# Reordering one store, one router step and the final gated sums of a mixture-of-experts tail

## The chip, the cores and the metric

The kernel runs on one core of a Trainium2 chip. The metric is the device time of one execution in microseconds (us), as the median of several runs. All times inside an execution are us from the start of its span.

## The reference

The program is one step of a diffusion trunk: one layer for 640 tokens (128 context tokens and 512 latent tokens) of width 1024, in fp32. Cut to what the change touches, the last part of the layer is:

```
h = modulate(x, norm_g[1], sh2, sc2)
scores = sigmoid(h @ w_router)                  # 16 experts, in 4 groups
idx, w = top 2 experts of the best group, weights normalised
for e in range(16):
    a = silu(h @ w_exp_gate[e]) * (h @ w_exp_up[e])
    y = y + combine[:, e] * (a @ w_exp_down[e])
x = x + g2 * y
return rms_norm(x, final_norm_g)
```

Ahead of it stand the input projection, the recurrent mixer, the neighbourhood attention, the merge of the two branches and the output projection.

## The kernel before

Every product is made in three passes: each operand is split into a high part (ScalarE, a rounding copy) and a low part (VectorE or GpSimd, the value less its high part), and TensorE multiplies high by high, high by low and low by high.

**The expert stage.** The 1280 (token, expert) pairs are sorted into tiles of 128 slots, one expert for each tile: 16 tiles for the 16 experts, and as many spill tiles as the routing asks for (`more` counts them in pairs). For each tile `t` three weight blocks of 2 MB are loaded: gate (`Wg`, index 0), up (`Wu`, index 1) and down (`Wd`, index 2). There is one raw buffer of each. SyncE issues the load of a block as soon as VectorE has made the low part of the block before it in that buffer (semaphore `W_lo_ok[x]`). GpSimd gathers the 128 token rows `hS` of a tile from DRAM. TensorE transposes them (`h_cols`), ScalarE makes the high part `hSH`, VectorE the low part `hSL` (`h_low`). TensorE then runs `up(t, 0)`, the transposes of the tile before it, `up(t, 1)` and `down(t-1)`. The result of a tile is weighted on ScalarE into `Ys` (with `wslot`, the weight of each slot), and SyncE stores it to the DRAM tensor `slot_rows` (`rows_out`, semaphore `ys_out`).

**Entry of the stage.** VectorE's queue, written out by hand, makes the low part of the first up block (`weights_low(1, 0)`), then `h_low(0, 0)`, then `slot_weights` (nine small operations: the slot weights, the slot of each token's two experts, the group of each slot), then the low part of the first down block.

**End of the stage.** The last two tiles are not stored. Their weighted rows `yg` are spread to the tokens by products on TensorE with one-hot matrices `mark`. All other tiles come back by gathers on GpSimd from `slot_rows`: for each of the five token tiles `G[t]` one gather of the row of the first expert (L680), and one that adds the row of the second expert (L685). GpSimd starts them when the low parts of the last up and down blocks are made (the `G` tiles lie in that memory) and when every `Ys` has been stored:

```
        pool.wait_ge(W_lo_ok[1], 2 * more + E)
        pool.wait_ge(W_lo_ok[2], 2 * more + (E - 1))
        for b in range(2):
            pool.wait_ge(ys_out[b], 16 * more + 8 * (E - 2))
```

SyncE's own queue at the end is: the last up block's load, the store of the last-but-one `Ys`, the store of the last `Ys` (`rows_out(2 * more + (E - 3), 1)`, which waits for ScalarE), the load of the last down block into the gate's buffer (L588, so it has the name `Wg` in the profile), the two broadcasts `g2b` of the gate rows, and then `fgb`, the broadcast of the final norm's weights, which waits for `gg_ok >= 1`, the first `G` tile multiplied by its gate. The five output stores follow.

**VectorE's last queue.** `out_low` and `out_half` make the weighted rows of the last tile and their low parts in two halves of the columns, with ScalarE's `ygH` between. TensorE's `spread(t, h)` adds the residual and the last two tiles' rows in PSUM. Then, for each token tile: `gated(t)` multiplies `G[t]` by the gate (it waits for both gathers of tile `t`), `summed(t)` adds PSUM, ScalarE squares and sums the row and takes the root, and `normed(t)` takes the reciprocal, scales by `fgb` and releases the store of the tile. `residual(4)` on TensorE reuses a PSUM bank and waits for `summed(0)`. SyncE and VectorE each work strictly through their queues in order: a wait holds everything behind it.

Of the kernel before, what the change touches and what calls it, by code (L numbers as in the profile page):

```python
# [32 lines left out]
TT = T // P  # L33
# [20 lines left out]
E, TOPK, SP_G = 16, 2, 4  # L54
# [53 lines left out]
def build(nc, xT, cT, w_ada, w_ada_late, b_ada, norm_g, final_g, wtiles, par_in, pack, biasd, w_router, r_bias,  # L108
# [15 lines left out]
    def sem(name):  # L124
        return ctx.enter_context(nc.semaphore(name))
# [220 lines left out]
    gg_ok, yg_ok, yh_ok, yl_ok, oc_mm = sem("gg_ok"), sem("yg_ok"), sem("yh_ok"), sem("yl_ok"), sem("oc_mm")  # L346
# [49 lines left out]
    def spill_pairs(engine):  # L396

        engine.wait_ge(idx_ok, 2)
        return engine.value_load(eI[0:1, NT:NT + 1], min_val=0, max_val=SPILL // 2)
# [32 lines left out]
    def _(sp):  # L432
# [131 lines left out]
        def rows_out(t, b):  # L564
            sp.wait_ge(ys_ev, t + 1)
            sp.dma_start(yd[bass.ds(t * P, P), :], Ys[b][:]).then_inc(ys_out[b], 16)

        def of_tile(t):
            return sp.value_load(eI[0:1, bass.ds(t, 1)], min_val=0, max_val=E - 1)

        def step(s, b, expert_of):
            load(0, s + 2, expert_of(s + 2))
            load(1, s + 2, expert_of(s + 2))
            if not (isinstance(s, int) and s == 0):
                load(2, s + 1, expert_of(s + 1))
                rows_out(s - 1, 1 - b)
# [4 lines left out]
        more = spill_pairs(sp)  # L581
        with nc.sync.Fori(0, more + (E // 2 - 2)) as j:
            for b in range(2):
                step(2 * j + 2 + b, b, of_tile)
        rows_out(2 * more + (E - 3), 1)
        sp.wait_ge(W_lo_ok[0], 2 * more + E)
        sp.sem_inc(ticks, 1)
        sp.dma_start(Wraw[0][:], experts[bass.ds(of_tile(2 * more + (E - 1)), 1), 2]  # L588
                     .rearrange("o p (k f) -> (o p) k f", k=KT)).then_inc(W_in[0], 16)

        sp.wait_ge(u_mm, 2 * more + (E - 1))
        sp.wait_ge(gb_in, 32)
# [813 lines left out]
    def _(dve):  # L1406
# [563 lines left out]
        def slot_weights():  # L1970

            dve.wait_ge(inv_mm, 2)
            w0, w1, w2 = (PS[:, 5, 160 + i * NT:160 + (i + 1) * NT] for i in range(3))
            st(v.tensor_copy(wslot[:], w2))
            st(v.tensor_tensor(slotF[:], posF.rearrange("p x t -> p (x t)"), tilF.rearrange("p x t -> p (x t)"), ALU.add))
            st(v.tensor_scalar(early_end[:], eF[:, NT:NT + 1], 2.0 * P, (E - 2.0) * P - 0.5, ALU.mult, ALU.add))
            seq.last(2)
            st(v.scalar_tensor_tensor(wslot[:], wslot[:], 1.0 / W_STEP, w1, ALU.mult, ALU.add))
            seq.last(2)
            st(v.tensor_scalar(wrest[:], slotF[:], -1.0, float(NT * P), ALU.mult, ALU.add))  # L1980
            seq.last(1)
            v.scalar_tensor_tensor(wslot[:], wslot[:], 1.0 / W_STEP, w0, ALU.mult, ALU.add).then_inc(idx_ok, 1)
            seq.last()
            st(v.scalar_tensor_tensor(wrest[:], slotF[:], early_end[:], wrest[:], ALU.is_ge, ALU.mult))
            st(v.tensor_scalar(groupI[:], idxF[:], float(NP), None, ALU.is_ge))
            seq.last()
            v.tensor_tensor(slotI[:].rearrange("p x t -> p (x t)"), slotF[:], wrest[:], ALU.add).then_inc(slot_ok, 1)

        def weights_low(x, t):

            for k in range(0, KT, 4):
                dve.wait_ge(W_hi_ok[x], 2 * t + (k // 4 + 1))
                y = v.tensor_tensor(W_lo[x][:, k:k + 4], Wraw[x][:, k:k + 4], W_hi[x][:, k:k + 4].bitcast(F32),  # L1993
                                    ALU.subtract)
            y.then_inc(W_lo_ok[x], 1)

        def h_low(t, b):
            dve.wait_ge(ht_hi, t + 1)
            v.tensor_tensor(hSL[b][:], PS[:, 0:2, :].rearrange("p h (k c) -> p (h k) c", k=4),  # L1999
                            hSH[b][:].bitcast(F32), ALU.subtract).then_inc(ht_lo, 1)  # L2000
# [48 lines left out]
                weights_low(2, t)  # L2049

        weights_low(1, 0)
        h_low(0, 0)
        slot_weights()
        weights_low(2, 0)
        expert(0, 0)
        expert(1, 1)
# [1 line left out]
        more = spill_pairs(dve)  # L2058
# [18 lines left out]
        def gated(t):  # L2077

            dve.wait_ge(gy_in[t], 32)
            v.tensor_tensor(G[t][:], G[t][:], g2b[min(t, 1)][:], ALU.mult).then_inc(gg_ok, 1)  # L2080

        def out_half(h):

            cols = slice(h * 512, (h + 1) * 512)
            dve.wait_ge(d_mm, 2 * more + (E + h))
            v.scalar_tensor_tensor(yg[1][:, cols], PS[:, 6 + h, :], ws2[:, 1:2], G2s[1][:, cols], ALU.mult, ALU.mult) \
                .then_inc(yg_ok, 1)

        def out_low(i, n, cols):

            dve.wait_ge(yh_ok, n)
            v.tensor_tensor(ygL[i][:, cols], yg[i][:, cols], ygH[i][:, cols].bitcast(F32), ALU.subtract) \
                .then_inc(yl_ok, 1)

        def summed(t):

            dve.wait_ge(oc_mm, t + 1)
            dve.wait_ge(gg_ok, t + 1)
            a = 2 * t % 8
            v.tensor_tensor(xo[t][:].rearrange("p (h c) -> p h c", h=2), PS[:, a:a + 2, :],  # L2100
                            G[t][:].rearrange("p (h c) -> p h c", h=2), ALU.add).then_inc(x2_ok, 1)

        def normed(t):

            if t == 0:
                dve.wait_ge(gb_in, 80)
            dve.wait_ge(sqo_ok, t + 1)
            st(v.reciprocal(stat[:, 10 + t:11 + t], stat[:, 5 + t:6 + t]))
            seq.last()
            v.scalar_tensor_tensor(yo[t][:], xo[t][:], stat[:, 10 + t:11 + t], fgb[:], ALU.mult, ALU.mult) \  # L2110
                .then_inc(out_ok, 1)

        out_low(0, 1, slice(0, D))
        dve.wait_ge(hs_in[1], 16 * more + 8 * E + 16)
        out_half(0)
        out_low(1, 2, slice(0, 512))
        out_half(1)
        out_low(1, 3, slice(512, D))
        for t in range(TT):
            gated(t)  # L2120
            summed(t)
            if t:
                normed(t - 1)
        normed(TT - 1)

    ctx.close()
# [89 lines left out]
```

## Time and profile before

| | |
|---|---|
| median of 3 runs | 1189.74 us (1188.63 to 1189.96) |
| time of the profiled execution | 1189.96 us |
| its span | 1188.1 us |
| TensorE matmul busy | 1128.4 us, 95% |
| VectorE busy | 914.0 us, 77% |
| ScalarE busy | 676.6 us, 57% |
| GpSimd busy | 265.2 us, 22% |
| granted TensorE clock, mean | 0.98 |
| DMA | 233.25 MB, 196 GB/s over the span |

The busy shares are means over stages that have different limits. The profiled execution's time is 1.86 us more than its span: what lies outside the span is taken as unchanged. The stages in order are the input projections and mixers, the merge and output projection, the router, the experts, and the tail of gathers and sums.

### The profile page before, as it was taken

How to read it: one execution, taken by the hardware profiler on the slowest of the kernel's cores; microseconds unless marked ns; L12 is line 12 of the kernel's file. 1: busy time of each engine (PE TensorE's matmuls, PEld its weight loads, DVE VectorE, ACT ScalarE, POOL GpSimd, SP SyncE). 2: the span in 40 equal slices, each digit the busy share in tenths (PEclk: the TensorE clock that was granted, in tenths of full speed). 3: DMA queues.
4: the chain of work that ended last, by engine and by line, in shares of the span. 5: the costliest groups of instructions: out<-in, count | busy, mean ns of one | idle time of the engine just before them, and what ended most of it. 6: DMA issues, size and time to landing. Idle time of an engine off the chain costs nothing.

```text
span 1188.1 us, 19988 instructions
## 1 busy us (share of the span) xinstructions
PE 1128.4 (95%) x7152; PEld 1029.3 (87%) x7152; DVE 914.0 (77%) x1276; ACT 676.6 (57%) x1038; POOL 265.2 (22%) x142
## 2 busy tenths in 40 slices
PE   5999999999999999999999999996899999999995
PEld 1599999999999998899999999995788888888873
DVE  5747797979788797866556655838798999999887
ACT  3646667576666757652222222436587787787753
POOL 0132122222122221133333332310111011011050
PEclk9999999999999999999999998997899999999998
DMA  9235612122121112124444435608899999999995
GB/s 367 101 98 154 197 59 81 46 77 70 66 84 58 62 57 80 41 90 142 142 142 141 141 106 213 236 18 333 300 342 403 415 424 419 424 409 411 415 318 170
DMA packets 54875, 233.25 MB, mean 196 GB/s; under 512 B 5368, under 2 KB 22048, under 8 KB 46368
## 3 DMA queue, kind: packets, MB, share of 16 engines
q1 hardware_dynamic: 50496, 216.79, 48.8%
q0 software_dynamic: 4320, 15.73, 4.0%
q8 instruction: 30, 0.49, 0.2%
q14 instruction: 29, 0.24, 0.1%
HBM read 211.50 MB, written 21.00 MB: 196 GB/s over the span
## 4 chain that ended last, share of the span: by engine, by line
PE 49%; DVE 4%; DMA 1%; issue 1%; ACT 1%; SPq 0%; DVEq 0%; ACTq 0%
PE PS L982 23%; PE PS L744 22%; PE PS L974 1%; PE PS L849 1%; PE PS L894 1%; DMA Wg<-in_experts 1%; DMA fgb<-in_final_g 1%; PE PS L995 1%; DVE hrow L1857 0%; DVE yo L2110 0%; DVE G L2080 0%; PE PS L882 0%; DVE WuLo L1993 0%; DVE WgLo L1993 0%; PE PS L900 0%
## 5 line engine op out<-in xcount | busy, mean ns | idle before, releaser
L622 POOL TENSOR_TENSOR wLo<-wRaw,wHi 128x1024 fp32r<-128x1024 f32 x80 | 202.7, 2534 | 549.5 <-ACT wHi L1095 549.5
L744 PE MATMUL PS<-hHi,wHi 128*128 128x320 f32 x896 | 285.6, 319 | 4.5 <-DVE hLo L1512 1.9
L744 PE MATMUL PS<-hLo,wHi 128*128 128x320 f32 x896 | 278.2, 310 | 0.0
L744 PE MATMUL PS<-hHi,wLo 128*128 128x320 f32 x896 | 278.1, 310 | 0.0
L744 PEld LDWEIGHTS PS<-hHi,wHi 128*128 128x128 f32 x896 | 169.9, 190 | 5.5 <-issue 5.2
L744 PEld LDWEIGHTS PS<-hLo,wHi 128*128 128x128 f32 x896 | 169.7, 189 | 0.0
L744 PEld LDWEIGHTS PS<-hHi,wLo 128*128 128x128 f32 x896 | 169.5, 189 | 0.0
L1681 DVE SCALAR_TENSOR_TENSOR acc<-adaL,csil,acc 128x512 f32<-128x512 f32 x112 | 103.9, 985 | 10.2 <-DMA adaL<-in_w_ada_late 9.7
L1095 ACT ACTIVATE wHi<-wRaw 128x1024 fp32r<-128x1024 f32 x80 | 84.1, 1051 | 45.2 <-PE PS L744 43.1
L1993 DVE TENSOR_TENSOR WgLo<-Wg,WgHi 128x2048 fp32r<-128x2048 f32 x34 | 76.3, 2287 | 15.2 <-ACT WgHi L1316 15.0
L1993 DVE TENSOR_TENSOR WdLo<-Wd,WdHi 128x2048 fp32r<-128x2048 f32 x34 | 76.3, 2287 | 8.5 <-ACT WdHi L1316 8.3
L1993 DVE TENSOR_TENSOR WuLo<-Wu,WuHi 128x2048 fp32r<-128x2048 f32 x36 | 80.8, 2285 | 1.4 <-ACT WuHi L1316 1.3
L1536 DVE TENSOR_TENSOR PtLo<-PS,PtHi 128x384 fp32r<-128x384 f32 (+1 forms) x80 | 39.6, 496 | 52.7 <-ACT PtHi L1131 52.6
L1316 ACT ACTIVATE WgHi<-Wg 128x2048 fp32r<-128x2048 f32 x34 | 63.3, 1910 | 17.4 <-DMA Wg<-in_experts 17.4
L1547 DVE TENSOR_SCALAR Sb<-Sb,prec 128x384 f32<-128x384 f32 (+1 forms) x80 | 70.6, 924 | 1.4
L1195 ACT ACTIVATE Sb<-Sb,nmax 128x384 f32<-128x384 f32 (+1 forms) x80 | 45.0, 564 | 46.5 <-DVE nmax L1559 46.4
L1316 ACT ACTIVATE WuHi<-Wu 128x2048 fp32r<-128x2048 f32 x36 | 66.9, 1909 | 3.9 <-DMA Wu<-in_experts 2.4
L1131 ACT ACTIVATE PtHi<-PS 128x384 fp32r<-128x384 f32 (+1 forms) x80 | 35.6, 445 | 57.0 <-PE PS L824 56.4
L644 POOL COPY idxc<-idxI 128x1 int32 (+1 forms) x16 | 15.1, 946 | 219.1 <-PE PS L974 219.1
L1316 ACT ACTIVATE WdHi<-Wd 128x2048 fp32r<-128x2048 f32 x34 | 63.1, 1906 | 0.3 <-DMA Wd<-in_experts 0.3
L982 PE MATMUL PS<-WgHi,hSH 128*128 128x512 f32 x144 | 57.4, 398 | 4.3 <-DVE hSL L1999 2.6
L982 PE MATMUL PS<-WuHi,hSH 128*128 128x512 f32 x144 | 57.8, 402 | 0.0
(358 smaller groups left out, 2822.6 us busy)
## 6 DMA issues: line engine op xcount, KB each, us to landing
wRaw<-in_wtiles SPq DMA_DIRECT2D x80, 512.0 KB, 3.5
Wu<-in_experts SPq DMA_DIRECT2D x18, 2048.0 KB, 9.5
Wg<-in_experts SPq DMA_DIRECT2D x18, 2048.0 KB, 10.6
Wd<-in_experts SPq DMA_DIRECT2D x17, 2048.0 KB, 10.3
adaL<-in_w_ada_late SPq DMA_DIRECT2D x32, 512.0 KB, 4.1
ada<-in_w_ada SPq DMA_DIRECT2D x8, 1024.0 KB, 17.7
slot_rows<-Ys SPq DMA_DIRECT2D x16, 512.0 KB, 11.0
slot_rows<-tab SPq DMA_DIRECT2D x12, 512.0 KB
```

What stands on the lines that cost most here:

```text
L622: nc.gpsimd.tensor_tensor(wLo[b][:], wRaw[b][:], wHi[b][:].bitcast(F32), ALU.subtract).then_inc(w_lo, 1)
L644: seq.step(nc.gpsimd.tensor_copy(idxc[b][:], idxI[:, bass.ds(t, 1)]))
L744: r = mm(PS[:, bank, 0:HALF], w[:, k, :], x[:, k, cols], start=(k == 0 and w is wHi[b] and x is xh), stop=(k == KT - 1 and w is wLo[b]))
L982: x = mm(out, lhs[l][:, k, :], rhs[r](k)[:, cols], start=(k == 0 and l == r), stop=(k == n - 1 and l == 1))
L1095: A(wHi[b][:], wRaw[b][:], ACT.Copy).then_inc(w_hi, 1)
L1131: A(PtHi[:, 0:nt, hh * P:(hh + 1) * P], PS[:, 6, 0:nt * P].rearrange("p (t q) -> p t q", q=P), ACT.Copy).then_inc(pt_hi, 1)
L1195: A(Sb[(blk + b) % 2][hh][:, 0:w], Sb[(blk + b) % 2][hh][:, 0:w], ACT.Exp, scale=-1.0, bias=nmax[hh][:], accum_out=psumr[:, hh:hh + 1]).th ...
L1316: A(W_hi[x][:, k:k + 4], Wraw[x][:, k:k + 4], ACT.Copy).then_inc(W_hi_ok[x], 1)
L1536: v.tensor_tensor(PtLo[:, 0:nt, cols], PS[:, 6, 0:nt * P].rearrange("p (t q) -> p t q", q=P), PtHi[:, 0:nt, cols].bitcast(F32), ALU.subtra ...
L1547: v.tensor_scalar(x, x, prec[:, hh:hh + 1], None, ALU.mult).then_inc(prob_ok, 1)
L1681: y = v.scalar_tensor_tensor(acc[:, g, :], w, c1, acc[:, g, :], ALU.mult, ALU.add)
L1993: y = v.tensor_tensor(W_lo[x][:, k:k + 4], Wraw[x][:, k:k + 4], W_hi[x][:, k:k + 4].bitcast(F32), ALU.subtract)
```

## The change

It moves instructions within three queues; it adds and removes no computation.

```
@@ SyncE, after the loop of the experts
-        rows_out(2 * more + (E - 3), 1)
         sp.wait_ge(W_lo_ok[0], 2 * more + E)
         sp.sem_inc(ticks, 1)
         sp.dma_start(Wraw[0][:], experts[bass.ds(of_tile(2 * more + (E - 1)), 1), 2]
                      .rearrange("o p (k f) -> (o p) k f", k=KT)).then_inc(W_in[0], 16)
+        rows_out(2 * more + (E - 3), 1)

@@ VectorE, entry of the expert stage
         weights_low(1, 0)
+        slot_weights()
         h_low(0, 0)
-        slot_weights()
         weights_low(2, 0)

@@ VectorE, summed(t)
             dve.wait_ge(oc_mm, t + 1)
-            dve.wait_ge(gg_ok, t + 1)
+            dve.wait_ge(gg_ok, TT)

@@ VectorE, the last queue (TT = 5)
         out_half(0)
+        gated(0)
         out_low(1, 2, slice(0, 512))
         out_half(1)
+        gated(1)
         out_low(1, 3, slice(512, D))
-        for t in range(TT):
+        for t in range(2, TT):
             gated(t)
+        summed(0)
+        for t in range(1, TT):
             summed(t)
-            if t:
-                normed(t - 1)
+            normed(t - 1)
         normed(TT - 1)
```

The load of the last down block is thus issued ahead of the last store of `Ys`; `slot_weights` runs ahead of the first `h_low`; all five `gated` run ahead of the first `summed`, two of them between the halves of the last tile's rows.

## Rows read from the trace of the kernel before

**Rows 1.** The page's first line.
```profile
span 1188.1 us, 19988 instructions
```

**Rows 2.** Chain that ended last, entry of the expert stage: start, us, engine, tile.
```profile
832.66 1.15 DVE hSL L1999
833.85 5.49 PE PS L982 x12
...
843.60 1.92 ACT WgHi L1316
...
850.18 5.73 PE PS L982 x24
```

**Rows 3.** Timeline of VectorE, entry of the expert stage.
```profile
833.71 0.17 DVE L1974 COPY wslot<-PS 128x26 f32<-128x26 f32 x1
...
834.68 4.49 DVE L1993 TENSOR_TENSOR WdLo<-Wd,WdHi 128x2048 fp32r<-128x2048 f32 x2
```

**Rows 4.** Windows, busy us; the last three columns are granted clock, DMA share, GB/s.
```profile
832.70:839.40 6.70, 5.55 (x14) 4.34 (x15) 6.43 (x12) 3.21 (x2) 0.98 (x2) 0.50 0.85 309
839.50:843.00 3.50, 3.50 (x21) 3.02 (x20) 1.23 (x1) 1.03 (x1) 1.16 (x2) 1.00 0.98 350
```

**Rows 5.** Chain that ended last, tail.
```profile
1136.92 8.01 DMA Wg<-in_experts
...
1154.16 5.74 PE PS L982 x24
...
1163.27 7.08 DMA fgb<-in_final_g
```

**Rows 6.** Timeline of SyncE's DMA issues, tail.
```profile
1124.61 11.10 SPq L566 DMA_DIRECT2D slot_rows<-Ys  x2
1136.92 0.35 SPq L588 DMA_DIRECT2D Wg<-in_experts  x1
```

**Rows 7.** Timeline of VectorE, tail.
```profile
1126.47 4.49 DVE L1993 TENSOR_TENSOR WgLo<-Wg,WgHi 128x2048 fp32r<-128x2048 f32 x2 [1.43 <-ACT WgHi L1316]
...
1137.02 4.49 DVE L1993 TENSOR_TENSOR WdLo<-Wd,WdHi 128x2048 fp32r<-128x2048 f32 x2
...
1171.77 1.22 DVE L2080 TENSOR_TENSOR G<-G,g2b 128x1024 f32<-128x1024 f32 x1
1173.09 1.22 DVE L2100 TENSOR_TENSOR xo<-PS,G 128x1024 f32<-128x1024 f32 x1
...
1180.80 1.23 DVE L2100 TENSOR_TENSOR xo<-PS,G 128x1024 f32<-128x1024 f32 x1
...
1183.57 0.16 DVE L2108 RECIPROCAL stat<-stat 128x1 f32<-128x1 f32 x1 [0.15 <-ACT stat L1402]
```

**Rows 8.** Timeline of GpSimd, tail: first gather, second and fifth adding gather.
```profile
1142.54 0.94 POOL L680 DMA_INDIRECT G<-slot_rows,slotI  x1 [10.75 <-issue]
...
1153.74 1.58 POOL L685 DMA_INDIRECT G<-slot_rows,slotI  x1 [0.30 <-issue]
...
1159.56 1.54 POOL L685 DMA_INDIRECT G<-slot_rows,slotI  x1 [0.30 <-issue]
```

**Rows 9.** Tile G, us from issue to landing: the issue at 1153.74.
```profile
DMA to landing us min/median/max: 7.9/7.9/7.9
```

**Rows 10.** Tile G, us from issue to landing: the issue at 1159.56.
```profile
DMA to landing us min/median/max: 10.5/10.5/10.5
```

**Rows 11.** DMA issues, us to landing: the `Ys` store at 1124.61.
```profile
slot_rows<-Ys SPq DMA_DIRECT2D x1, 512.0 KB, 11.0
```

**Rows 12.** DMA issues, us to landing: the `Ys` store at 1135.36.
```profile
slot_rows<-Ys SPq DMA_DIRECT2D x1, 512.0 KB, 2.8
```

**Rows 13.** Windows of the tail before the gathers, columns as in rows 4.
```profile
1132.20:1137.90 5.70, 5.70 (x27) 4.73 (x26) 5.70 (x4) 4.80 (x4) 0.00 (x0) 1.00 0.72 285
1138.00:1142.50 4.50, 4.50 (x23) 3.70 (x23) 4.50 (x4) 1.85 (x3) 0.00 (x0) 1.00 0.92 346
```

**Rows 14.** DMA queues between 1142.5 and 1146.5: packets, MB, share of 16 engines.
```profile
q1 hardware_dynamic: 261, 1.26, 92.0%
```

More of the change, by code:

```diff
@@ L584, in _ @@
                 step(2 * j + 2 + b, b, of_tile)
-        rows_out(2 * more + (E - 3), 1)
         sp.wait_ge(W_lo_ok[0], 2 * more + E)
@@ L589, in _ @@
                      .rearrange("o p (k f) -> (o p) k f", k=KT)).then_inc(W_in[0], 16)
+        rows_out(2 * more + (E - 3), 1)
         sp.wait_ge(u_mm, 2 * more + (E - 1))
@@ L2051, in _ @@
         weights_low(1, 0)
+        slot_weights()
         h_low(0, 0)
-        slot_weights()
         weights_low(2, 0)
@@ L2097, in summed @@
             dve.wait_ge(oc_mm, t + 1)
-            dve.wait_ge(gg_ok, t + 1)
+            dve.wait_ge(gg_ok, TT)
             a = 2 * t % 8
@@ L2115, in _ @@
         out_half(0)
+        gated(0)
         out_low(1, 2, slice(0, 512))
         out_half(1)
+        gated(1)
         out_low(1, 3, slice(512, D))
-        for t in range(TT):
+        for t in range(2, TT):
             gated(t)
+        summed(0)
+        for t in range(1, TT):
             summed(t)
-            if t:
-                normed(t - 1)
+            normed(t - 1)
         normed(TT - 1)
```

## The prediction

> **What bounds the kernel now.** The page gives the span [rows 1]: the profiled execution took 1189.96 us for 1188.10 us of span, 0.22 us above the median of the runs shown. I then followed the chain of work that ended last through the two places that the change touches. At the entry of the expert stage it runs from VectorE's `hSL` to TensorE, to the weight split on ScalarE, its low part on VectorE, and back to TensorE at 850.18 [rows 2]. From there TensorE is the chain, without a gap of note, to about 1134. In the tail the chain leaves TensorE: it goes through the load of the last down block, 24 products, and then the load of `fgb`, which lands at 1163.27 + 7.08 = 1170.35 [rows 5]. After that VectorE works almost without pause to the end. Hidden just behind `fgb` lies a second limit, which the chain does not name: the last adding gather, issued at 1159.56, lands 10.5 us later, at 1170.06 [rows 8, 10]. That one decides what the change can give.
>
> **Part 1, `slot_weights` ahead of `h_low`.** The nine small operations start at 833.71 and the next block starts at 834.68: 0.97 us [rows 3]. Their inputs are there, so no wait is added. What is queued behind them is now `hSL`, and TensorE waits for `hSL` [rows 2]. What they give back is nothing: the slot weights and slots are not used until much later, and the low part of the down block starts at the same time in either order. The delay goes on: TensorE's first product of the tile ends later, so does ScalarE's tanh, the split of the next gate block that stands behind it at 843.60, its low part, and TensorE's restart at 850.18 [rows 2]. From there TensorE has no slack in which to lose it. Price: +0.97 us on everything after.
> This price has two ends. TensorE ran at half clock from 832.7 to 839.4 (granted 0.50, that is 1.2 GHz) and at full clock (2.4 GHz) from 839.5 [rows 4], and before this it had stood still waiting for `hSL`. If the clock rises at the same moment although TensorE starts 0.97 us later, the lost 0.97 us are lost at half rate, and the price is 0.49 us. If the longer stop makes the stretch at half clock half as long again (3.35 us, a bound that I set), another 1.7 us of work is lost: 2.2 us. I take 0.97, and keep 0.5 and 2.2.
> The Trainium skill, page "TensorE: Matmul & The Clock Gate", Part 1, says that the throttled clock is the default and that activity releases it. By that the rise moves with TensorE's start, and the price is the whole 0.97 us; the trace's rise after a busy stretch is in line with it, and does not prove it.
>
> **Part 2, the load ahead of the store on SyncE.** The last store of `Ys` held SyncE until 1124.61 + 11.10 = 1135.71, and the load went out 1.21 us later, after the register load of the expert's number [rows 6]. Without the store it waits only for the low part of the gate block, done at 1126.47 + 4.49 = 1130.96 [rows 7], so it goes out at 1130.96 + 1.2 = 1132.2 us, 4.7 us earlier. By its 8.01 us [rows 5] it lands near 1140.2 in place of 1144.93. The split and the low part of this block, then the last transposes and the restart of TensorE at 1154.16 [rows 5], come earlier by something between 1 and 4.4 us; TensorE first has to finish the down product of the tile before. None of this is on the path of the end, as the gathers land later.
> What it does to the path is in the DMA queue. Between 1132.2 and 1137.9 the DMA engines were 72% busy, between 1138.0 and 1142.5 92% [rows 13]. Moving the load forward fills 0.28 x 5.7 = 1.6 us and 0.08 x 4.5 = 0.4 us of that idle time: SyncE's queue is done 2.0 us earlier. In 1142.5 to 1146.5 that queue held 92% of the engines although the first gather had been issued at 1142.54 [rows 8, 14]; so the gathers start to move 2.0 us earlier, and as they come one behind the other, the last lands at 1170.06 - 2.0 = 1168.06. Ends: 0 (the gathers have a delay of their own and don't use the gap), and 4.7 us (the whole advance of the load).
> The store of `Ys` is now behind 2 MB. It is issued near 1135.4 as before, the load lands near 1140.2, and a store of a quarter of its size adds a quarter of what the load moves in, 8.01/4 = 2.0 us at most, 1.3 us if it goes at the load's own rate without its fixed part. I take 1141.5 for its landing. GpSimd waits for the low part of the last down block too, which ends at 1137.02 + 4.49 = 1141.51 [rows 7] and is not touched by the change. A tie: the gathers are issued at 1142.54 as before. `g2b` follows the store and is first used by `gated(0)`.
>
> **Part 3, the order of the last sums.** `fgb` was waited for until 1170.35 because SyncE loads it after `gated(0)`. Now `gated(0)` runs between the two halves of the last tile's rows, ahead of where it stood, and `fgb` lands well before it is used: this limit is gone. The new one is `gated(4)`: every `summed` and `normed` now stands behind it, and it waits for the last adding gather. Call its landing L. From L: `gated(4)` takes 1.32 us to the start of the next (1171.77 to 1173.09), `summed(0)` 1.22, and from the end of `summed` to the reciprocal ScalarE needs 1183.57 - 1182.03 = 1.54 us [rows 7]: normed(0) starts at L + 4.08. Before, from normed(0) at 1170.37 (0.02 after `fgb`) to the end of the span was 17.73 us, with three `gated` in it; without them 17.73 - 3 x 1.32 = 13.77. The span ends at L + 17.85. For L = 1168.06 that is 1185.9, 2.2 us before 1188.10; the break-even is L = 1170.25, so that with L where it was, 0.2 us are gained.
> `gated(0)` and `gated(1)` stand before `ygL`, which TensorE waits for. The second adding gather landed at 1153.74 + 7.9 = 1161.64 [rows 8, 9], now near 1159.6; `gated(1)` ends near 1160.8 and the last `ygL` about when it did before. TensorE's remaining products of the tail end before VectorE asks for them, since VectorE asks only after L: cost nothing. If the cover is gone (L under 1165), this stall is next. `residual(4)` now waits for `summed(0)`, done at L + 2.5 = 1170.6; it is wanted for `summed(4)` some 8 us later.
>
> **Sum.** 1188.10 + 0.97 - 2.2 = 1186.9 of span, 1.2 us less; on the median of the runs shown, 1189.74 - 1.2 = 1188.5 us. A measurement of this kernel can hardly tell less than 0.2%, which is 2.4 us, from no change, so this is no change.
>
> **Rivals.**
> (a) The gathers gain more: with the whole 4.7 us L = 1165.4, the span ends 4.9 us earlier before the entry's price, and the net is -3.9 us (1185.8). For it: SyncE's queue is what stood in front of the gathers [rows 14]. Against: the engines have only 2.0 us of idle time to give [rows 13]. It is over 0.2% from L = 1166.9 on at the full price of part 1, or L = 1167.4 at its half. Chance 0.20.
> (b) The end gains nothing, because the gathers keep their landing of 1170.06: -0.2 + 0.97 = +0.8 us, 1190.5. The change of order is then without use. Chance 0.10.
> (c) The clock stays at half after the longer stop: 2.2 - 2.2 = 0, 1189.7. Against it stands that TensorE was busy 5.55 of the 6.70 us [rows 4] and still would be for most of them. Chance 0.08.
> (d) Slower: the store of `Ys` sits behind the load. A store issued right behind a 2 MB load took 11.0 us to land against 2.8 us for one alone [rows 11, 12]. At 11.0 us it lands at 1146.4 and GpSimd starts its gathers at 1147.4, 4.9 us late; the queue ahead is then empty, which gives back the 2.0 us and, by the 92% of the 4 us [rows 14], about 1 us more. L = 1172, the span ends at 1189.8, and with part 1 the net is +2.7 us (1192.4). It decides from a landing of the store after 1141.5. Against it: the store at 1124.61 had another full block in front of its load, this one has not. Chance 0.07.
> The Trainium skill, page "DMA: Bandwidth & Descriptors", section on queues, rings and completion order, says that on each engine the descriptors of a ring are consumed in order, so a store cannot pass a load issued before it. Rows 11 and 12 agree (11.0 against 2.8 us); by this rule the store lands after the load in any case, which is what (d) rests on.
> The likeliest is the sum above, with a range of its own of 1187.4 to 1189.7: chance 0.55.
>
> **How the numbers follow.** Faster by over 0.2%: (a), 0.20. Slower by over 0.2%: most of (d), 0.06. The rest, 0.74, is within 0.2%. The range of 1186.2 to 1190.9 holds the likeliest, (b), (c) and the nearer half of (a); it leaves out (d) and the far half of (a).
>
> **What would show it.** After the change: the first product of the experts starts near 834.8 and TensorE's restart after it near 851.1 (or 850.7 if the clock rises when it did); the last load is issued near 1133 and lands near 1141, both with part 1's delay; the gathers are issued near 1143.5; the chain of waits in the tail no longer has `fgb` in it, and VectorE stops before `gated(4)` for the last gather, near 1169; from there to the end are 17.9 us. I am wrong if the first gather is issued later than about 1144, if VectorE does not stop before `gated(4)`, or if the restart of TensorE near 851 does not move by the nine operations' time.

## The result: slower by 0.55%, and the profile after

The changed kernel takes 1195.04 us at the median of 20 runs, the kernel before 1188.84 us at the median of 20; the ratio is 1.0055, with a 95% interval of 1.0037 to 1.0074, or 6.5 us (4.4 to 8.8). I had forecast no change, 1188.5 us with a range of 1186.2 to 1190.9. The profiled execution took 1194.78 us for a span of 1192.9 us, 4.8 us more than before.

The entry of the expert stage in the chain of the changed kernel, against [rows 2]:

```profile
833.86 1.15 DVE hSL L1999
835.05 5.49 PE PS L982 x12
...
844.72 1.92 ACT WgHi L1316
...
851.30 5.74 PE PS L982 x24
```

`hSL` and everything behind it is 1.1 to 1.2 us late, of which 0.17 us came from earlier stages. The windows, against [rows 4]:

```profile
833.60:840.30 6.70, 5.25 (x12) 4.02 (x13) 5.76 (x4) 2.56 (x2) 0.97 (x1) 0.50 0.95 344
840.50:844.00 3.50, 3.50 (x21) 3.02 (x20) 1.23 (x1) 1.03 (x1) 1.16 (x2) 1.00 0.93 343
```

The stretch at half clock (1.2 GHz) is as long in this pair of executions. The other profiles of the old entry have a shorter one (below, on the clock). The tail in the chain, against [rows 5]:

```profile
1136.88 8.39 DMA slot_rows<-Ys
1145.29 0.80 issue
1146.09 3.00 POOL G L680
1149.09 0.30 issue
1149.39 2.50 POOL G L680
...
1163.60 11.43 DMA G<-slot_rows,slotI
1175.05 1.24 DVE G L2080
```

Neither the load nor `fgb` is in it. The chain now runs through the store of `Ys`, which took 8.39 us to land, through GpSimd's gathers and the last adding gather to `gated(4)`. SyncE's issues, against [rows 6]:

```profile
1133.57 0.33 SPq L587 DMA_DIRECT2D Wg<-in_experts  x1
1136.88 0.35 SPq L566 DMA_DIRECT2D slot_rows<-Ys  x1
```

The times from issue to landing of the last three transfers ahead of this store in SyncE's queue: the down block issued at 1125.62, the store of the `Ys` before it, issued at 1126.15, and the last load, issued at 1133.57.

```profile
Wd<-in_experts SPq DMA_DIRECT2D x1, 2048.0 KB, 10.5
slot_rows<-Ys SPq DMA_DIRECT2D x1, 512.0 KB, 12.5
Wg<-in_experts SPq DMA_DIRECT2D x1, 2048.0 KB, 10.4
```

VectorE, against [rows 7]:

```profile
1162.89 1.23 DVE L2080 TENSOR_TENSOR G<-G,g2b 128x1024 f32<-128x1024 f32 x1 [4.59 <-DMA G<-slot_rows,slotI]
...
1175.05 1.23 DVE L2080 TENSOR_TENSOR G<-G,g2b 128x1024 f32<-128x1024 f32 x1 [1.89 <-DMA G<-slot_rows,slotI]
...
1188.42 0.17 DVE L2108 RECIPROCAL stat<-stat 128x1 f32<-128x1 f32 x1 [0.15 <-ACT stat L1402]
```

VectorE waits 4.59 us before `gated(0)`, between the halves of the last tile's rows, and for four of the five `gated` in all. The last of them starts at L = 1163.60 + 11.43 = 1175.03, 5.0 us later than L was before (1170.06).

**One ruler for all profiles.** An execution may come to the router several us early or late: the operation that makes `ohW`, just ahead of the first edited line, starts between 820.5 and 833.6 in the fourteen profiles below. So single spans can't be compared, and I cut each profile into three pieces, all in us. The entry goes from the start of `ohW` to the end of the second gate block's low part (what TensorE's restart waits for), the loop from there to ScalarE's last `Ys`, and the tail from there to the end of the span. L (the landing of the last adding gather) and the first gather's issue are counted from the start of that `Ys` as well. All are differences of two starts or ends in the timelines.

```
kernel                     entry   loop    tail   first gather     L
before                     22.75  284.01  54.06       8.50      36.0
after                      23.70  284.42  57.33      10.52      39.5
e1  part 2                 21.54  283.97  56.84      10.70      41.3
e2  part 1                 23.51  283.95  53.99       8.48      36.1
e3  part 3                 21.50  284.00  55.42       8.48      37.5
e4  parts 1, 3             23.62  284.78  54.34       8.48      36.5
e11 parts 2, 3             21.58  283.98  59.54      10.67      41.6
e5  after, store on ACT    23.68  283.98  59.61      10.69      41.8
e6  after, slivers         23.58  283.98  53.93       9.81      36.0
e10 after, stop filled     21.22  284.26  60.61      12.74      42.7
e7  before, fgb early      21.49  283.98  51.74       8.48      35.6
e8  best of edits          21.49  283.96  50.62      10.25      38.0
e9  e8, stop filled        20.16  283.98  51.03      11.62      38.4
e12 before, stop filled    20.18  283.98  54.19       8.48      36.0
```

For the pair of before and after: 0.95 of entry, 0.41 of loop, 3.27 of tail and 0.17 ahead of the entry make the 4.8 us.

### The profile page after: what moved, and what is told of

It reads as the page before. It is cut to its first block, busy times and chain, and to the rows that moved or that the text cites. A ratio compares the mean times of both kernels' runs of the same rounds, so it can differ in the third digit from the quotient of the medians.

```text
span 1192.9 us, 19988 instructions
## 1 busy us (share of the span) xinstructions
PE 1129.4 (95%) x7152; PEld 1028.8 (86%) x7152; DVE 913.8 (77%) x1276; ACT 676.6 (57%) x1038; POOL 272.0 (23%) x142
## 4 chain that ended last, share of the span: by engine, by line
PE 48%; DVE 3%; DMA 2%; POOL 1%; issue 1%; ACT 1%; POOLq 0%; SPq 0%; DVEq 0%; ACTq 0%
PE PS L982 23%; PE PS L744 22%; PE PS L974 1%; PE PS L849 1%; DMA G<-slot_rows,slotI 1%; DMA slot_rows<-Ys 1%; POOL G L680 1%; PE PS L894 1%; PE PS L995 1%; DVE hrow L1857 0%; POOL G L685 0%; DVE WuLo L1993 0%; DVE WgLo L1993 0%; PE PS L882 0%; DVE xo L2100 0%
## 5 line engine op out<-in xcount | busy, mean ns | idle before, releaser
L1131 ACT ACTIVATE PtHi<-PS 128x384 fp32r<-128x384 f32 (+1 forms) x80 | 35.6, 445 | 59.7 <-PE PS L824 55.7
L644 POOL COPY idxc<-idxI 128x1 int32 (+1 forms) x16 | 19.6, 1224 | 217.2 <-PE PS L974 217.2
```

Of the source, the lines that this page charges most:

```text
L644: seq.step(nc.gpsimd.tensor_copy(idxc[b][:], idxI[:, bass.ds(t, 1)]))
L1131: A(PtHi[:, 0:nt, hh * P:(hh + 1) * P], PS[:, 6, 0:nt * P].rearrange("p (t q) -> p t q", q=P), ACT.Copy).then_inc(pt_hi, 1)
```

## The experiments

Timed ones ran beside the kernel before on the same chip; the interval of a ratio is about 0.25% to each side. e6 and e10 ran once, for their profiles, and have no ratio. The profiles, read by the pieces above, tell more than the times; each is one execution.

### The three parts alone

Part 2 alone (e1) is the first hunk of the change, part 1 alone (e2) the second, part 3 alone (e3) the last two. e4 is the changed kernel with the first hunk undone:

```
+        rows_out(2 * more + (E - 3), 1)
         sp.wait_ge(W_lo_ok[0], 2 * more + E)
...
-        rows_out(2 * more + (E - 3), 1)
```

> Only the load ahead of the store (part 2), the rest as before. Theory A (the late gathers cost only together with the new order of the sums): the store lands about 8 us after its issue, the first gather goes out near 1145 in place of 1142.5, the last adding gather lands near 1173.5, but in the old order only gated(4) stands behind it; fgb again lands near 1171 and the end is at most 1.5 us later than before. Rival B (part 2 alone makes the loss): 3 to 5 us later than before.

Measured: ratio 1.0017 (0.9990 to 1.0043); tail 56.84 us, 2.8 us over before. Its chain:

```profile
1138.27 8.56 DMA slot_rows<-Ys
1147.66 3.00 POOL G L680
1150.96 2.49 POOL G L680
...
1158.11 7.98 DMA G<-slot_rows,slotI
1166.12 1.24 DVE G L2080
1167.42 8.60 DMA fgb<-in_final_g
1176.04 0.17 DVE stat L2108
```

Theory A was right on the gathers and wrong on the end. The last gather lands 5.3 us later (41.3 against 36.0) and is indeed hidden in the old order. But `fgb` is not: its load waits for `gated(0)`, `gated(0)` waits for the first pair of gathers, and so the delay comes back through `fgb`. Part 2 alone costs nearly 3 us of tail, by either order of the sums.

> Only slot_weights ahead of the first h_low (part 1). Both theories of the tail: +1 us over before, with TensorE's first product and its restart later by 1.0 to 1.2 us. Rival C (the entry costs more, by the clock of TensorE): 2 us or more, with a longer stretch of granted clock 0.5 at the entry.

Measured: ratio 1.0021 (0.9999 to 1.0042); tail as before. Entry 23.51 us. That is 0.8 us over the profile of before, but 2.0 us over e1 and e3, which have the old entry: see the clock, below.

> Only the new order of the final sums (part 3). Theory A: store and gathers as before (first gather near 1142.5, last landing near 1170), so the end is L + 17.9, between -1 and +0.5 us from before. Rival D (part 3 alone makes the loss, by its stall between the two halves of yg): 3 us or more over before.

Measured: ratio 1.0022 (0.9997 to 1.0047); first gather as before, L = 37.5, tail 55.42, which is L + 17.9. So the stall in the middle (rival D) is not it: the tail is 1.4 us longer, because L is 1.5 us later in this execution and nothing hides it any more.

> The changed kernel with the store ahead of the load again (parts 1 and 3). Theory A: the store lands within 3 us of its issue, the gathers start 3.5 us earlier than in the changed kernel, and the time is before's + 1 us, that is 4 to 5 us below the changed kernel. Rival D: the changed kernel's time stays.

Measured: ratio 1.0017 (0.9992 to 1.0041) against the changed kernel's 1.0055; tail 54.34, 3.0 us below the changed kernel's. The store is the difference:

```profile
1141.24 0.94 POOL L680 DMA_INDIRECT G<-slot_rows,slotI  x1 [11.07 <-issue]
```

This is 8.48 us after `Ys` (1132.76), against 10.5 us in the changed kernel. I had expected 3.5 us of difference, and it is 2.0. L is 36.5, and the tail again L + 17.9.

Parts 2 and 3 together, part 1 undone (e11):

```
         weights_low(1, 0)
-        slot_weights()
         h_low(0, 0)
+        slot_weights()
```

> The changed kernel with slot_weights behind h_low again (parts 2 and 3 alone). If the parts of the loss add, the entry is back at 21.5 us from ohW (or 22.7 in the clock's other phase), the tail stays near 57 us from Ys, and the time is about 2 us below the changed kernel and 3 to 4 us over before. Rival: the tail takes up the entry's gain and the time stays at the changed kernel's.

Measured: ratio 1.0039 (1.0011 to 1.0067), 1.9 us below the changed kernel's 1.0055, with intervals that overlap; entry 21.58, tail 59.54. The entry is back, and the tail is the worst kind: L = 41.6, to which 17.9 are added. With after (57.33) and e10 (60.61) the tail of parts 2 and 3 together stands in three profiles at 59.2 in the mean, 5.1 us over the 54.1 of before, e2 and e12. e10 has an edit of its own that lengthens it (below); without it the mean is 58.4, 4.4 us over.

### Why the store lands late

The changed kernel with the store issued by ScalarE, on that engine's own DMA queue (e5):

```
 SyncE
-        rows_out(2 * more + (E - 3), 1)
 ScalarE, behind the loop of the experts
+        act.wait_ge(ys_ev, 2 * more + (E - 2))
+        act.dma_start(yd[bass.ds((2 * more + (E - 3)) * P, P), :], Ys[1][:]).then_inc(ys_out[1], 16)
```

> The changed kernel, but the last store of Ys is issued by ScalarE on its own DMA queue, after the split of the last up-to-date down block (about 4 us after Ys is made), so it is not behind the 2 MB load in a queue. Theory E (the store's place behind the load in one queue delays the gathers): it lands within about 4 us of its issue, about 8 us after Ys starts against 9.7 us now; the first gather goes out 8.5 us after Ys starts as in the kernel before, and the end comes 2 to 3 us earlier than in the changed kernel. Rival F (the DMA engines are simply full, whichever queue holds the store): the store lands 9 us or more after Ys starts and nothing is gained.

Measured: ratio 1.0056 (1.0030 to 1.0082). The issue went out right behind `Ys`, 1.31 us after it starts, not 4 us: it left at 1129.50, while the first of the two splits ahead of it in ScalarE's queue ran (1129.20 to 1131.11), and before the second began. The chain:

```profile
1129.50 8.55 DMA slot_rows<-Ys
1138.08 0.80 issue
1138.88 3.01 POOL G L679
1141.89 0.30 issue
1142.19 2.49 POOL G L679
```

8.55 us on a queue of its own, against 8.39 behind the load in one queue: theory E fell, and rival F came as it said. One reservation: the two `g2b` broadcasts (1 MB) went out 4.3 us earlier here (counted from `Ys`) and stood ahead of the store too. So a queue of its own did not help, but that only the amount already with the DMA engines counts, and not the queue, is not shown. In the changed kernel they were 97% busy from 1132.2 to 1143.9:

```profile
1132.20:1143.90 11.70, 11.70 (x55) 9.68 (x54) 11.17 (x8) 8.26 (x7) 0.48 (x1) 1.00 0.97 370
```

against 72% and 92% before [rows 13]. The load took 10.4 us in place of 8.01 and was there 8.4 us after `Ys` starts against 10.9: a gain of 2.5 us for 4.9 us of earlier issue. The store behind it pays for it with 5.6 us.

### Why the gathers slow down as well

Two gather issues of the changed kernel take 3.00 and 2.50 us, the other plain ones 0.94 (those that add take 1.5 to 1.9). I had seen such rows before the prediction and not asked. In the kernel before, GpSimd and VectorE:

```profile
1147.51 2.49 POOL L680 DMA_INDIRECT G<-slot_rows,slotI  x1 [0.30 <-issue]
1150.31 3.13 POOL L685 DMA_INDIRECT G<-slot_rows,slotI  x1 [0.30 <-issue]
```

```profile
1146.90 2.29 DVE L2005 TENSOR_TENSOR WgLo<-Wg,WgHi 128x2048 fp32r<-128x2048 f32 x1 [4.20 <-ACT WgHi L1367]
...
1149.71 2.28 DVE L2005 TENSOR_TENSOR WgLo<-Wg,WgHi 128x2048 fp32r<-128x2048 f32 x1
```

Each long issue overlaps one of the two low parts of the last down block. It also ends with it: in the thirteen profiles with these low parts at full size, all twenty issues of plain gathers (L680, without an add) that meet one take 2.1 to 3.0 us and end 0.81 or 0.82 us after it, as here 1147.51 + 2.49 = 1150.00 against 1146.90 + 2.29 = 1149.19. e6 is the changed kernel with these two cut to 16 of every 512 columns, which leaves most of that low part out:

```
-            return v.tensor_tensor(W_lo[0][:, k:k + 4], Wraw[0][:, k:k + 4], W_hi[0][:, k:k + 4].bitcast(F32),
+            return v.tensor_tensor(W_lo[0][:, k:k + 4, 0:16], Wraw[0][:, k:k + 4, 0:16],
+                                   W_hi[0][:, k:k + 4, 0:16].bitcast(F32), ALU.subtract)
```

> The changed kernel with VectorE's two last low parts of the last down block cut to 16 of 512 columns (this part of the computation is left out). Theory G (GpSimd's writing of gather descriptors stands still while VectorE makes a low part of a block): the first two gather issues take 0.94 us each in place of 3.00 and 2.50, the fifth is done 3.6 us earlier, the last adding gather lands 1 to 3 us earlier. Rival H (the issues are long because the DMA queue is full): they stay at 2.5 to 3 us.

Measured, GpSimd and VectorE of e6:

```profile
1146.88 0.94 POOL L680 DMA_INDIRECT G<-slot_rows,slotI  x1 [13.10 <-DMA slot_rows<-Ys]
1148.12 0.94 POOL L680 DMA_INDIRECT G<-slot_rows,slotI  x1 [0.30 <-issue]
```

```profile
1146.78 0.23 DVE L2005 TENSOR_TENSOR WgLo<-Wg,WgHi 128x64 fp32r<-128x64 f32 x1 [1.06 <-ACT WgHi L1367]
```

All five plain ones are 0.94 us. Theory G holds. L is 36.0 in place of 39.5 and the tail 53.93 in place of 57.33, although the gathers still start 9.8 us after `Ys`; 0.7 us of the 3.4 is this earlier start (10.5 in the changed kernel). Some of the tail's gain may come from VectorE's shorter work itself; that L moved is read from the gathers alone.

So the late store did its harm twice: it started the gathers 2 us late, and it put their very first issues beside VectorE's low parts, where before only the fifth and sixth met them. The second harm is not in the issues themselves: from the first to the last they take 17.0 us before and 17.5 after. It is in how little the DMA engines had to do meanwhile. The same 14 us, from 8.4 us after `Ys` on, in before, after and e6, and 2 us of after:

```profile
1142.50:1156.50 14.00, 12.73 (x55) 9.61 (x54) 9.58 (x12) 5.38 (x4) 11.83 (x8) 1.00 0.94 317
1144.00:1158.00 14.00, 14.00 (x61) 10.62 (x60) 10.68 (x13) 5.38 (x4) 10.09 (x6) 1.00 0.65 225
1145.50:1159.50 14.00, 14.00 (x61) 10.65 (x60) 6.70 (x13) 4.70 (x4) 10.18 (x9) 1.00 0.88 267
1147.00:1149.00 2.00, 2.00 (x11) 1.65 (x10) 2.00 (x3) 0.75 (x1) 2.00 (x1) 1.00 0.01 4
```

Before, the long issues came when four gathers were already with the engines, and these stayed busy (94%). After, the engines had done what was queued by 1147, while the first gather's issue (1146.09 to 1149.09) still waited, and stood idle: 65%, or 4.1 us of idle time more. L is 3.4 us later. e1 and e11 have 61% and L 5.3 and 5.6 us later, e4 has 89% and e6 88%, with L 0.5 and 0.0 us later.

The Trainium skill, page "SBUF — State Buffer", section on the two separate sides, says that GpSimd can't write the descriptors of its DMAs while VectorE holds the port pair that the two share. It names for this VectorE's two-port modes, and against a GpSimd operation that reads SBUF an operation with two SBUF inputs, which these low parts are. The trace is in line with this: a plain gather, which reads its indices `slotI` from SBUF, takes 0.94 us to issue beside no such operation, 2.1 to 3.0 us beside one of 2.29 us, and ends 0.8 us after it. Which of the issue's own accesses waits is not shown.

### The clock at the entry

Entries with `h_low` first: 22.75 in before, and 21.54, 21.50, 21.58, 21.49, 21.49 in the others. Entries with `slot_weights` first: 23.70, 23.51, 23.62, 23.68, 23.58. The gap is 0.95 us in the pair of before and after, and 2.1 us otherwise. In e11 (old entry):

```profile
828.90:832.10 3.20, 2.94 (x7) 2.36 (x8) 3.17 (x11) 2.41 (x2) 0.88 (x1) 0.50 0.97 307
832.30:835.50 3.20, 3.20 (x20) 2.72 (x19) 2.18 (x1) 1.02 (x1) 0.20 (x2) 1.00 0.96 402
```

TensorE is at half clock for its first products and at full clock (2.4 GHz) from 832.3 on. In e2 (new entry) it is at half clock in both stretches of the same place:

```profile
835.00:838.40 3.40, 1.55 (x4) 1.27 (x5) 3.37 (x7) 2.96 (x2) 0.97 (x1) 0.51 0.87 255
838.50:841.80 3.30, 3.30 (x9) 2.53 (x9) 2.69 (x2) 0.00 (x0) 0.00 (x0) 0.50 0.93 385
```

The first 12 products tell the same: 4.3 to 4.4 us in e1, e3, e7, e8 and e11, but 5.3 to 5.5 us in before, after, e2, e4, e5 and e6.

To see whether TensorE's stop is the cause, e12, e9 and e10 fill it with extra transposes into a PSUM bank that holds nothing (20 in e12 and e9, 28 in e10):

```
         h_cols(0, 0, 16)
+        for _ in range(20):
+            nc.tensor.transpose(PS[:, 7, 0:P], C("ident"), C("ident"))
         expert(0, 0, 16)
```

> The kernel before with 20 extra transposes in TensorE's wait and nothing else. Theory K: 1 to 2 us faster than before. Rival L: no difference.

Measured: entry 20.18, no half clock after the stop, the first 12 products in 3.0 us where before had 5.49:

```profile
829.80:833.00 3.20, 2.88 (x13) 2.31 (x13) 3.17 (x11) 2.58 (x2) 0.97 (x1) 1.00 0.93 287
```

```profile
830.22 3.04 PE PS L982 x12
```

The mechanism of theory K holds in the profile. In the time it doesn't show: ratio 1.0009 (0.9981 to 1.0036), which a gain of 1.3 us (21.5 less 20.2, 0.11%) can't be told from.

> The changed kernel with 28 such extra transposes. Theory K: its first 12 products take 3 to 4.4 us in place of 5.3 to 5.5, and the stretch from ohW to the low part of the second gate block falls from 23.6 to 22.5 us or less. Rival L: it stays at 23.6 us.

Measured: entry 21.22. So with the clock at full in both, `slot_weights` first costs 21.22 - 20.17 = 1.05 us, its own length; the other 1.1 us of its price are the clock. But the tail of e10 is the longest, 60.61: counted from `ohW`, `Ys` starts 2.6 us sooner than in after (305.5 against 308.1), but the store lands only 0.4 us sooner (317.4 against 317.8), and the gathers started 12.74 us after `Ys`.

### Can it be better than both?

In the kernel before, `fgb` waits for `gated(0)`, though its memory is free from the last low part of `Wd` on. e7 removes that wait and lets `fgb` count on another semaphore, on which `normed(0)` waits:

```
-        sp.wait_ge(gg_ok, 1)
-        sp.dma_start(fgb[:], final_g.broadcast_to([P, D])).then_inc(gb_in, 16)
+        sp.dma_start(fgb[:], final_g.broadcast_to([P, D])).then_inc(h2_pre, 16)
```

> The kernel before, with fgb loaded as soon as its memory is free (no wait for gated(0)), on a semaphore that DVE's other waits don't use. Theory I (fgb, landing at Ys + 36.3 us, sets the end of the kernel before, and the last gather only just hides behind it): the idle time of VectorE before normed(0) of 2.3 us goes, the end comes 1.5 to 2.5 us earlier. Rival J (its 0.5 MB delay the gathers by the same 1.3 us ahead of them and the order of the sums needs them): within 0.5 us.

Measured: ratio 0.9987 (0.9968 to 1.0007); tail 51.74, 2.3 us below before. The chain no longer has `fgb`:

```profile
1146.71 5.78 PE PS L981 x24
...
1157.02 1.22 DVE xo L2099
1158.24 1.14 DVE G L2079
...
1160.62 0.16 DVE stat L2107
```

Theory I holds in the profile, and the ratio can't be told from no change; L is 35.6, so its 0.5 MB ahead of the gathers did not delay them.

e8 adds to e7 part 2 and the store on ScalarE's queue (as in e5), e9 adds the filled stop to that.

> The kernel before with three edits: the last down load is issued first (part 2), the last store of Ys goes on ScalarE's DMA queue, fgb is loaded early; the sums and slot_weights keep their old order. Theories E and I together: the gathers start 8.5 us after Ys starts, VectorE runs its sums without a wait from gated(0) on, the end is 2.5 to 4 us earlier than before. Rival F: the gathers start 2 us late, the first gated waits, and the end is between -1 and +1 us.

Measured: ratio 0.9984 (0.9963 to 1.0005); tail 50.62, 3.4 us below before, although the gathers start at 10.25 as rival F had it; the end that F gave, within 1 us of before, did not come. Against e5 (tail 59.61) two things differ. From L to the end are 12.6 us and not 17.9: in the old order of the sums only `gated(4)` needs the last gather. And L is 38.0 in place of 41.8, which is not explained here.

> The kernel before with the last down load first, the last store of Ys on ScalarE's queue, fgb early, and 20 extra transposes of the identity into an unused PSUM bank behind the first h_cols, in the time in which TensorE waits for the first hSL. Theory K (TensorE's stop there sets how long the half clock lasts): no stretch at half clock after the first product, the first 12 products take 2.8 to 3.5 us in place of 4.4 or 5.5, and the time is 1 to 2 us below the run with the other three edits. Rival L (the half clock comes anyway): no difference.

Measured: ratio 0.9969 (0.9946 to 0.9993), the only kernel here that is faster than before beyond its interval: entry 20.16, tail 51.03. The interval ends just short of 1, and this is one of ten ratios of experiments, so it is weak evidence by itself. Against e8 it is 0.15% less (1.8 us, as theory K had it), with intervals that overlap.

## Why the prediction was wrong

**The step that failed** is in part 2: "By its 8.01 us it lands near 1140.2", and from it "I take 1141.5 for its landing". The load took 10.4 us. The store landed 1.3 us behind it, which is within what I had for the store itself (1.3 to 2.0), at 1145.27, 9.7 us after `Ys` starts where 1141.5 stood for 7.5. So it was the load's time that was mis-sized. The 8.01 us was the time of a load that had one store of 0.5 MB in front of it; the moved load had the rest of the down block in front (landing at 1136.1) and the store of the `Ys` before (1138.7). I had also said that the engines had only 2.0 us of idle time to give; a load that is issued 4.7 us earlier can then land about 2.0 us earlier, not 4.7 (it was 2.5), and the store behind it lands after that. Both numbers stood in the prediction and contradict each other. The "tie" of 1141.5 with 1141.51 came from the wrong one: GpSimd waited for the store, to 1145.29, and the first gather went out at 1146.09, past the 1144 that I had set as a sign of being wrong.

**What it set off** I had as rival (d), at 0.07: the store behind the load, gathers late, L = 1172, 2.7 us slower. The mechanism is shown by e4 against after (store first: first gather 8.48 in place of 10.5 us after `Ys`, tail 3.0 us less). Its size was 3 to 5 us of tail. In (d) the store landed even later, at 1146.4, and yet its L, 38.0 us after `Ys`, came out 1.5 to 4.7 us too early. It gave back 3 us of the gathers' late start because the queue ahead would be empty. Nothing came back: in after the first gather is 2.0 us later and L 3.4, since the engines stood idle beside the first two issues, which I had not priced. In e6, without these low parts, L is 3.4 us earlier again, 0.7 of it by an earlier start. My reason against (d), that this load had no full block in front of it, did not hold: it had the transfers above, and the engines were 97% busy.

**"The gathers start to move 2.0 us earlier"** rested on the same wrong landing: they start when the store has landed. L was forecast at 1168.06, 34.0 us after `Ys`, and came at 39.5.

**Part 1.** The mechanism was right: nine operations of 0.97 us on the path; e10 against e12 and e9 gives 1.05. I took this as the price and had 2.2 us as its upper end, by a longer half clock; rival (c) stood at 0.08. Five profiles of each entry say that the upper end, 2.1 us, is the rule; the profile of before, a sixth of the old entry, was the exception. My reason against it was that TensorE was busy for most of the stretch; that holds for after too (5.25 of 6.70 us), and the half clock was longer in all five all the same.

**Part 3.** `fgb` left the path, as said, and the end is L + 17.85: measured 1192.9 - 1175.03 = 17.87, and 17.9 in e3, e4, e10 and e11. The stall of `gated(0)`, which I had at nothing, was 4.59 us; it is not in the chain, since L was later still.

**The sum.** Entry +2.1 and tail +5.1 (the means above) make 7.2 us, or 6.5 with the 4.4 us that leave e10 out; the whole time says 6.5 (4.4 to 8.8). That the three parts alone measure 0.17 to 0.22% each does not tell their shares; the tails do: part 2 alone 2.8, part 3 alone 0.3 to 1.4 (e4, e3), both together 5.5 (e11).

**What stays open.** Why the clock rose later in the profile of before than in the five others of the old entry. Why the last adding gather lands after 11.4 us in one profile of the new kernel and 12.4 in two others, and where the 13 us come from by which executions differ ahead of the router. How the DMA engines share themselves between queues when full was not separated from what stood ahead of the store in e5.

## What to carry to other kernels

A transfer issued earlier into busy DMA engines gains little more than the idle time that they had (here 4.9 us of earlier issue gave 2.5 us, with 2.0 us of idle time), and what is issued behind it loses (5.6 us): move the small store that someone waits for ahead of the large load that nobody waits for yet. Before all work is put behind the last of several arrivals (`gg_ok >= TT`), read how far apart they land: here the old order kept 5 us of a late gather off the path (e8 ends at L + 12.6, the new order at L + 17.9). And look at what the engines have to do while a gather's issue waits: two slow issues left them 94% busy behind four others, and 65% as the first ones. And one profile shows one course of the clock: a price that has a half clock in it needs several.

## What the runs showed of the hardware

- A plain gather's issue on GpSimd that takes 0.94 us takes 2.1 to 3.0 us beside a VectorE subtraction of 128x2048 fp32 from two SBUF inputs (2.29 us) and ends 0.81 or 0.82 us after it (twenty issues in thirteen profiles). It takes 0.94 us again when the subtraction is cut to 0.23 us (e6).
- A 0.5 MB store on a queue of its own took 8.55 us to land beside 3 MB of loads that were issued before it, as long as behind a load in one queue (8.39, with 2 MB of load ahead), and 2.8 us when it was issued ahead of the load [rows 12].
- TensorE's stop of 2.5 to 2.6 us before the first `hSL` was followed by 12 products in 4.3 to 4.4 us in five profiles and 5.5 us in one; after a stop 1 us longer (3.5 us) they took 5.3 to 5.5 us in all five. With the stop filled by extra transposes they took 3.0 us (e12).
